# Attention block of a hybrid decoder layer: five query tiles one after another, where three were interleaved

## The reference, cut to what matters

```
s  = relu(qi @ ki^T)                       # 16 index heads of width 64
sc = sum_h wi[h] * s[h];  causal           # index score of each key
idx = top_k(sc, 128)                       # 128 keys are kept per query
p  = softmax(q @ k^T + bias[distance])     # 4 heads of width 128, kept keys only
o_a = p @ v
x  = x + concat(o_a, o_b, o_c) @ w_out     # this block does the o_b, o_c rows
```

## Time and profile before

| | us |
|---|---|
| median of 3 runs | 3632.32 (3630.06 to 3635.02) |
| profiled execution | 3625.24 |
| its span | 3623.4 |
| this block in the trace | 1682 to 1943.7 |
| attention on DVE | 1719.7 to 1943.7 |

### The profile page before, as it was taken

How to read it: one execution, slowest core, us unless ns; L and a number is a source line. 1 busy time by engine, 2 the same in 40 slices (tenths; PEclk the granted TensorE clock), 3 DMA queues, 4 the chain that set the end, 5 groups by cost and what they waited for, 6 DMA issues and landing times. The chain is left out here.

```text
span 3623.4 us, 54272 instructions
## 1 busy us (share of the span) xinstructions
PE 3210.1 (89%) x22287; PEld 2955.0 (82%) x22287; DVE 2186.9 (60%) x3229; ACT 564.8 (16%) x1074; POOL 1419.0 (39%) x853
## 2 busy tenths in 40 slices
PE   7978997999993477783997999999999999999998
PEld 6935886899772377752886999999999999999998
DVE  7025994898318666446896755546555555555554
ACT  3222211122325211114321200000000000000000
POOL 4353332476323232313333444434444343444442
PEclk9989998999995698776998999999999999999999
DMA  5322332478643000217333222322323222222232
GB/s 181 95 78 83 107 88 77 128 218 253 204 143 102 17 1 1 54 51 206 96 99 135 67 91 83 94 83 85 91 82 94 82 91 83 87 85 89 83 94 97
DMA packets 415941, 360.30 MB, mean 99 GB/s; under 512 B 26362, under 2 KB 367962, under 8 KB 414309
## 3 DMA queue, kind: packets, MB, share of 16 engines
q1 hardware_dynamic: 379664, 287.06, 27.0%
q0 software_dynamic: 13440, 42.02, 3.6%
q10 hardware_dynamic: 22592, 27.59, 2.3%
HBM read 311.63 MB, written 46.20 MB: 99 GB/s over the span
## 5 line engine op out<-in xcount | busy, mean ns | idle before, releaser
L3067 POOL TENSOR_TENSOR om_ring<-om_raw,om_mask 128x1024 fp32r<-128x1024 f32 x264 | 680.7, 2579 | 937.2 <-DVE om_ring L3185 937.2
L3107 PE MATMUL om_ps<-om_h,om_ring 128*128 128x272 f32 x6144 | 780.3, 290 | 21.6 <-issue 18.1
L3107 PEld LDWEIGHTS om_ps<-om_h,om_ring 128*128 128x128 f32 x6144 | 777.6, 190 | 24.1 <-issue 23.9
L3107 PE MATMUL om_ps<-om_hid,om_ring 128*128 128x272 f32 x6144 | 770.6, 288 | 0.0
L3107 PEld LDWEIGHTS om_ps<-om_hid,om_ring 128*128 128x128 f32 x6144 | 769.8, 188 | 0.0
L3185 DVE CAST om_ring<-om_mask 128x1024 fp32r<-128x1024 f32 x264 | 455.2, 1724 | 9.1
L321 POOL TENSOR_TENSOR w_ring<-w_raw,w_mask 128x1024 fp32r<-128x1024 f32 (+2 forms) x110 | 259.5, 2378 | 370.5 <-DVE w_mask L452 210.3
L372 PE MATMUL pm_ps<-h,w_ring 128*128 128x280 f32 x2688 | 363.7, 297 | 26.2 <-issue 11.5
L372 PEld LDWEIGHTS pm_ps<-h,w_ring 128*128 128x128 f32 x2688 | 356.0, 193 | 33.7 <-issue 26.6
L3193 DVE TENSOR_TENSOR om_x<-om_x,om_ps 128x272 f32<-128x272 f32 x288 | 112.7, 433 | 357.8 <-PE om_ps L3107 354.5
L390 PE MATMUL pq_ps<-w_ring,h 128*128 128x512 f32 (+2 forms) x1440 | 291.3, 364 | 7.7 <-POOL w_ring L321 7.6
(11 more groups left out here) (521 smaller groups left out, 3668.9 us busy)
## 6 DMA issues: line engine op xcount, KB each, us to landing
om_raw<-in_w_up SPq DMA_DIRECT2D x128, 512.0 KB, 4.1
om_raw<-in_w_down SPq DMA_DIRECT2D x128, 512.0 KB, 3.6
w_raw<-in_w_in SPq DMA_DIRECT2D x112, 512.0 KB, 3.8
ao_raw<-in_w_out SPq DMA_DIRECT2D x32, 384.0 KB, 4.0
as_qb<-q_rows SPq DMA_DIRECT2D x32, 256.0 KB
projT<-pm_stage ACTq DMA_DIRECT2D x56, 140.0 KB
conv_x<-projT SPq DMA_DIRECT2D x28, 280.0 KB, 2.7
xT_scratch<-ln_xT SPq DMA_DIRECT2D x1, 4480.0 KB, 15.4
```

Of the source, the lines that this page charges most:

```text
L3067: pool.tensor_tensor(f32r(ring[:, s, 1, half_of(q)]), raw[:, q, :], mask[:, q, :], ALU.subtract).then_inc(split[q], 1)
L3107: ins = pe.matmul(ps[bank][:, 0:HM], w, f32r(src[:, b, k, kept_half(half)]), start=first, stop=last)
```

## The change

Attention goes through the tiles in sequence: on DVE the head sums of tile i, then its 16 selection rounds, then its four heads, then tile i + 1. The due times come from three tables of step lengths. The tile's phases begin at:

| tile | sums | selection | heads | next tile |
|---|---|---|---|---|
| 0 | 12 | - | 12 | 21 |
| 1 | 21 | 29 | 45 | 54.4 |
| 2 | 54.4 | 64.3 | 84.3 | 95.3 |
| 3 | 95.3 | 107.3 | 131.3 | 143.9 |
| 4 | 143.9 | 146.9 | 170.9 | 184.3 |

The index scores on PE are due 2.5 before the sums, the logits matmuls 2.5 before their use on DVE. The projection's streams keep their due times. Instructions, shapes and buffers are the same; only the order changes, on DVE, PE, ACT and POOL.

```diff
-AS_FROM, AS_PER = (12.0, 24.0, 50.5, 89.0, 122.5, 156.0), (0.75, 1.65, 2.4, 2.1, 2.1, 3.0)
+SUM_PER, TOP_PER, HEAD_PER = (0, 0.5, 0.62, 0.75, 0), (0, 1.0, 1.25, 1.5, 1.5), (1.5, 1.6, 2.0, 2.4, 2.6)
+SUM_FROM, TOP_FROM, HEADS_FROM = {}, {}, {}
+CLOCK = 12.0
+for TILE in range(5):
+    SUM_FROM[TILE] = CLOCK
+    TOP_FROM[TILE] = SUM_FROM[TILE] + HI * SUM_PER[TILE] + 3 * (TILE == 4)
+    HEADS_FROM[TILE] = TOP_FROM[TILE] + (TOPP // 8 * TOP_PER[TILE])
+    CLOCK = HEADS_FROM[TILE] + 4 * HEAD_PER[TILE] + 3
 def logits_at(i, h):
-    return when(0, 4 * h + 1.2) if i == 0 else when(i + 1, 4 * h + 1.7) if i < 4 else when(5, 1 + h)
+    return HEADS_FROM[i] + 2 + HEAD_PER[i] * h
 def weights_at(i, h):
-    return logits_at(i, h) + (1.5 if i == 0 else 2.8 if i == 4 else 2 * AS_PER[i + 1])
+    return logits_at(i, h) + HEAD_PER[i] + 0.5
...
-                    for r in range(TOPP // 8):
-                        yield when(i, r)
-                        step(dve.max(best[0:n, r % 2, :], x))
-                        step(dve.match_replace(x, best[0:n, r % 2, :], x, TAKEN))
-                        if i < 3:
-                            add_head(i + 1, r)
...
-                        if i >= 2 and r % 4 == 1:
-                            yield logits_at(i - 1, r // 4)
-                            logits(i - 1, r // 4)
-                        if i >= 2 and r % 4 == 3:
-                            yield weights_at(i - 1, r // 4)
-                            normalise(i - 1, r // 4)
...
+                    if i in (1, 2, 3):
+                        for h in range(HI):
+                            yield SUM_FROM[i] + SUM_PER[i] * h
+                            add_head(i, h)
+                            if h == 12:
+                                heads_out(i - 1)
+                    if i:
+                        for r in range(TOPP // 8):
+                            yield TOP_FROM[i] + TOP_PER[i] * r
+                            step(dve.max(best[0:n, r % 2, :], x))
+                            step(dve.match_replace(x, best[0:n, r % 2, :], x, TAKEN))
...
+                    yield logits_at(i, 0)
+                    logits(i, 0)
+                    for h in range(HA):
+                        if h + 1 < HA:
+                            yield logits_at(i, h + 1)
+                            logits(i, h + 1)
+                        yield weights_at(i, h)
+                        normalise(i, h)
```

More of the change, by code:

```diff
@@ L1737, in in_time @@
         due[who] = next(streams[who], None)
-AS_FROM, AS_PER = (12.0, 24.0, 50.5, 89.0, 122.5, 156.0), (0.75, 1.65, 2.4, 2.1, 2.1, 3.0)
+SUM_PER, TOP_PER, HEAD_PER = (0, 0.5, 0.62, 0.75, 0), (0, 1.0, 1.25, 1.5, 1.5), (1.5, 1.6, 2.0, 2.4, 2.6)
 FIRST_UNIT, UNIT = 2.0, 10.6
-def when(phase, r):
-    return AS_FROM[phase] + AS_PER[phase] * r
+SUM_FROM, TOP_FROM, HEADS_FROM = {}, {}, {}
[5 more added lines that the diff above has]
+    CLOCK = HEADS_FROM[TILE] + 4 * HEAD_PER[TILE] + 3
 def unit_at(n):
@@ L1796, in attend_and_project @@
         wide = ((0, slice(0, WIDE)), (1, slice(WIDE, TP)))
-        order = [(when(0, h) - 2.5, "i", 1, h) for h in range(HI)]
-        order += [(when(i - 1, h) - 2.5, "i", i, h) for i in (2, 3) for h in range(HI)]
-        order += [(when(3, 5), "w", 4, 0), (when(3, 6.5), "w", 4, 1), (when(3, 9), "s", 4, 0)]
+        order = [(SUM_FROM[i] + SUM_PER[i] * h - 2.5, "i", i, h) for i in (1, 2, 3) for h in range(HI)]
+        order += [(SUM_FROM[4] - 1.5, "w", 4, 0), (SUM_FROM[4] - 0.5, "w", 4, 1), (SUM_FROM[4] + 1.8, "s", 4, 0)]
         order = sorted(order + [(logits_at(i, h) - 2.5, "h", i, h) for i in range(5) for h in range(HA)])
@@ L2157, in inputs @@
                     step(dve.tensor_scalar(wi[0:NT[i], i, :], wi[0:NT[i], i, :], float(HI * DI) ** -0.5, None, ALU.mult))
-                yield when(1, 2)
+                yield SUM_FROM[2]
                 dve.wait_ge(s["wq_in"], 16 * 8)
@@ L2207, in attend @@
             def attend():
[L2208 to L2218, removed]
@@ L2219, in attend @@
-                for i in range(1, 5):
+                for i in range(5):
                     n = rows[i]
                     x = sc[0:n, i % 3, 0:keys[i]]
-                    for r in range(TOPP // 8):
-                        yield when(i, r)
-                        step(dve.max(best[0:n, r % 2, :], x))
-                        step(dve.match_replace(x, best[0:n, r % 2, :], x, TAKEN))
-                        if i < 3:
-                            add_head(i + 1, r)
[L2228 to L2238, removed]
-                        if i >= 2 and r % 4 == 1:
-                            yield logits_at(i - 1, r // 4)
-                            logits(i - 1, r // 4)
-                        if i >= 2 and r % 4 == 3:
-                            yield weights_at(i - 1, r // 4)
-                            normalise(i - 1, r // 4)
-                    step(dve.tensor_scalar(x, x, TAKEN, NEG, ALU.not_equal, ALU.mult))
-                    diag = sc[0:n, i % 3, P * i:keys[i]]
-                    dve.tensor_tensor(diag, diag, causal[0:n, 0:n], ALU.add).then_inc(s["mask_ready"], 1)
@@ L2248, in attend @@
[L2248 to L2256, removed]
+                    yield SUM_FROM[i] + 2.9 * (i == 4)
+                    if i == 0:
+                        dve.tensor_copy(sc[:, 0, 0:P], causal[:, :]).then_inc(s["mask_ready"], 1)
@@ new lines, in attend @@
+                    if i == 4:
+                        dve.wait_ge(s["score"], nth["s", 4, 0] + 1)
+                        dve.wait_ge(s["bm_ready"], HA * 2)
+                        for ps, part in both(("s", 4, 0)):
+                            ins = dve.tensor_copy(sc[0:TAILP, 1, part], ps[0:TAILP, 0:WIDE])
+                        ins.then_inc(s["sums_out"], 1)
+                        dve.wait_ge(s["sums_out"], 1)
+                        step(dve.tensor_tensor(x[:, 512:], x[:, 512:], causal[0:TAILP, 0:TAILP], ALU.add))
@@ new lines, in attend @@
+                    if i in (1, 2, 3):
[9 more added lines that the diff above has]
+                            step(dve.match_replace(x, best[0:n, r % 2, :], x, TAKEN))
+                            if i == 4 and r == 2:
+                                heads_out(3)
+                        step(dve.tensor_scalar(x, x, TAKEN, NEG, ALU.not_equal, ALU.mult))
+                        diag = sc[0:n, i % 3, P * i:keys[i]]
+                        dve.tensor_tensor(diag, diag, causal[0:n, 0:n], ALU.add).then_inc(s["mask_ready"], 1)
```

## The result

The changed kernel takes 3654.6 us (median of 5 runs) against 3632.3 (5 runs): ratio 1.0059, interval 1.0048 to 1.0071, so **22.3 us slower**. I had forecast slower by 9.3 us (3641.6). The sign held and so did the range (3629 to 3655), its upper end by 0.4 us; the size was 2.4 times too small.

A forecast was written before the change was run, and what follows sets the result against it. PE and DVE, both nearly full, bounded the block together; in sequence each phase takes its slower engine's time. Phases and tail summed to 233.3 us against 224.0, +9.3 on the 3632.32 median: 3641.6, range 3629 to 3655.

The forecast's parts named there:

- the walk: Step through PE's and DVE's lists over the attention block: 233.3 us instead of 224.0, +9.3; chance 0.48.
- DVE's stop at tile 4: DVE stands about 9 us at its wait for tile 4's sums (L2232).
- the first rival: PE's lead absorbs DVE's lag after selections 1 to 3, saving up to 11 us; 3625 to 3636; chance 0.32.
- the signs that I had named: Trace checks, including DVE's selection 4 starting at 1908 and PE's last weights about 10 us earlier than 1940.
- the tail: After selection 4 only tile 4's heads remain: 17.1 us to the end; bounds 13 with overlap, 20 at lower clock.
- the second rival: PE's stops at four phase changes lower its clock, 2 to 3 us each; tail's PE steps double; 3654; chance 0.13.
- Heads 0 with sums 1: Block start, tile 0's heads then tile 1's head sums: +9.8 and +13.4 us on DVE.
- Heads 1: Tile 1's heads after its selection: +10.4 us, PE waiting 1.3 at the third logits, 0.7 and 1.6 at turns.
- heads 2: Tile 2's heads after its selection: +10.8 us, with PE waiting 2.9 and 1.3.
- The rule weighed in the prediction: Shared DVE/POOL SBUF ports: lows add up to 1.4 us to first normalise of tiles 1 and 2; total about +11.
- Selection 3: Tile 3's selection rounds, bound by DVE: 24.2 + 3.4 (masks and adds of two units) + 0.7 = 28.3 us.
- Heads 3 with tile 4's scores: Tile 3's heads and tile 4's scores: +26.7 us, PE waiting 3.3 and 5.0 behind the lows of unit 13.

The follow-up runs named there:

- e3: Changed kernel with projection weights planned unevenly, more in selections and fewer in sums and heads; ratio 1.0023 to the kernel before, attention 231.3 us against 246.2.
- e4: Changed kernel with tile i-1's heads back between tile i's selection rounds, sums still a separate phase; ratio 1.0013 to the kernel before, attention 227.2 us.
- e1: Changed kernel plus 84 unread weight matmuls on PE between the last weights and tile 4's heads; ratio 1.0046 to the kernel before, attention 242.2 us.
- e8: e1 plus 2, 3 and 5 unread matmuls before the third logits matmul of tiles 1, 2 and 3; ratio 1.0048 to the kernel before, attention 244.2 us.
- e6: e3 with POOL's bm of tiles 1 to 4 due 2.4 earlier; ratio 1.0045 to the kernel before, attention 238.4 us.
- e7: e4 with projection weights paced by phase, at other rates than e3; ratio 1.0013 to the kernel before, attention 226.9 us.
- e9: Changed kernel with POOL's lows of unit 13 moved ahead of tile 3's first bm; ratio 1.0059 to the kernel before, attention 243.9 us.

## Why the prediction was right, and where its size failed

**What held.** The model: phases with waits on both sides, each as long as its slower engine. Of the eleven windows, five came within 0.2 us of the walk: selections 1, 2 and 4 (17.9, 24.0, 28.0 for 18.0, 24.1, 27.9) and sums 2 and 3 (20.0 and 26.5 for 20.1 and 26.7). So did DVE's stop at tile 4 (9.1 for 9). PE does wait at the third logits matmul; the first rival, that its lead takes up the lag, asked for no wait there after selections 1 to 3 and is refuted by 10.5 us of it. e3 shows the sums to be PE's, e4 shows that phases of heads cost most of the loss.

Not all of this is skill. PE's waits up to the end of heads 3 come to 18.0 us for 16.6 in the walk, but in other places: 10.5 for 7.5 at the third logits matmuls, 3.7 for 8.6 at the turns of tiles 1 to 3, 3.4 for 0.5 in heads 0, and 0.4 at a relu. And two of the signs that I had named failed. Selection 4 starts at 1914.9 (1922.5 less 7.6), 6.9 us after 1908, and PE ends its weights at 1938.0, where I had 1931.

**What failed is a term of the sum: the tail**, 17.1 in the walk, 20 at the lower clock as its bound, and 23.0 in the trace. That is 5.9 of the 12.9 us that are missing. I had written that PE would end the weights early, that is, that it would stand before the tail, and had kept the price of the clock for the second rival and as a bound. It belonged in the walk, since PE's early end was part of it. e1 gives 3.9 us for the clock and e8 2.0, each a part of its price. The 2.0 by which e1's tail still exceeds the walk lie behind the last normalise, 5.4 us for about 3.5. There the last turn waits 1.3 us behind the values of the head before, a place in PE's list that I had not counted; the last values take 2.26 at the lower clock where I had 1.8; and four unread matmuls stand between. How much the order alone costs in the changed kernel no run separates.

The second rival named two places for the clock. It was right about the tail ("PE steps double") and, as far as the runs show, wrong about the size at the changes of phase, 2 to 3 us each: heads 1 gained 0.7 and heads 2 nothing on the changed kernel when their clock was full. Its time, 3654, is the measured one, by luck; half of its reason is not.

**Smaller terms** make up the rest. Their reasons are read from rows, and no experiment tests one by itself:

- Heads 0 with sums 1, +1.7. I gave 16 scores their weights and forgot that PE has tile 0's turns and values among them, 4 x 0.34 us by my own prices; that is the likely reason.
- Heads 1, +1.1, and heads 2, +1.4. Heads 1 in order of time, DVE beside POOL, and PE before its first turn:

```profile
1770.10 1.56 DVE L2129 TENSOR_SCALAR ao_mask<-ao_raw 128x768 uint32<-128x768 uint32 x2
1770.26 1.98 POOL L2103 TENSOR_TENSOR mix<-ao_toe,ao_sc 128x256 f32<-128x256 f32 x2 [7.63 <-DVE ao_sc L2239]
...
1772.21 3.61 POOL L2088 TENSOR_TENSOR ao_ring<-ao_raw,ao_mask 128x768 fp32r<-128x768 f32 x2
...
1774.04 1.93 DVE L2203 TENSOR_SCALAR mix<-mix,ao_den 128x256 f32<-128x256 f32 x1
...
1775.03 1.92 PE L1938 MATMUL ao_w<-ao_mh,ao_ring 128*128 128x272 f32 x6
...
1776.75 0.47 PE L1988 MATMUL ao_t<-ident,mix 128*128 128x128 f32 x2
...
1778.34 0.35 DVE L2203 TENSOR_SCALAR mix<-mix,ao_den 128x256 f32<-128x256 f32 x1
```

  The normalise takes 1.93 beside the lows and 0.35 without them, and the masks 1.56 beside `bm` where they take 1.03. I had allowed 0.5 for each. The rule weighed in the prediction (the Trainium skill, SBUF — State Buffer, "Who interferes with whom"), which asked for up to 1.4 more, agrees with this. But the delay was not what the first turn waited for. The normalise ended at 1775.97, and the turn came at 1776.75, behind six weights that took 1.92 at the lower clock. In e1, with the clock at 1.00, they took 1.10; the turn then waited 0.60 for the equally slow normalise, and heads 1 was 10.7. So of the 1.1, some 0.7 is the clock. In heads 2 the first normalise took only 0.75, but the masks before the second `logits` took 1.70 instead of 1.03. That is about half of the 1.4, and I have no experiment on the rest; e8, with the clock at 1.00 there, is no shorter.
- Selection 3, +0.9. The walk counted masks and adds of two units in it. The trace has three pairs of masks (at 1865.8, 1878.1 and 1890.4, 1.03 us each) and two pairs of adds, so one pair of masks more.
- Heads 3 with tile 4's scores, +2.3. The rows in order of time:

```profile
1893.63 1.27 POOL L2103 TENSOR_TENSOR mix<-ao_toe,ao_sc 128x512 f32<-128x512 f32 x1 [11.00 <-DVE ao_sc L2239]
1894.86 3.59 POOL L2088 TENSOR_TENSOR ao_ring<-ao_raw,ao_mask 128x768 fp32r<-128x768 f32 x2
...
1895.68 1.41 PE L1973 MATMUL ao_s<-ao_att 128*128 128x512 f32 x2 [4.45 <-DVE mix L2189]
...
1898.41 3.74 POOL L2103 TENSOR_TENSOR mix<-ao_toe,ao_sc 128x512 f32<-128x512 f32 x3
...
1899.72 0.69 DVE L2189 TENSOR_TENSOR mix<-ao_s,mix 128x512 f32<-128x512 f32 x1 [3.38 <-POOL mix L2103]
...
1902.49 0.66 PE L1988 MATMUL ao_t<-ident,mix 128*128 128x128 f32 x4 [2.68 <-DVE mix L2203]
...
1903.67 3.43 PE L1938 MATMUL ao_w<-ao_mh,ao_ring 128*128 128x272 f32 x12
...
1913.73 1.78 PE L1938 MATMUL ao_w<-ao_mh,ao_ring 128*128 128x272 f32 x12
```

  The order `bm`, lows, `bm` is as predicted, and the two waits of PE are 4.45 and 2.68 where I had 3.3 and 5.0: together less. What was missing is behind them: twelve weights take 3.43 us just after PE's waits and 1.78 ten us later. Some 1.6 us of clock lie there, in front of the next turn. That is read from the rows, and e8, whose clock stayed at 0.88 in this phase, does not test it.

**Where 22.2 us went**, then: 9.3 as the walk had it, 5.9 in the tail (2.0 to 3.9 of it clock, at the least), 7.0 in the smaller terms, for most of which the rows offer a reason. By cause instead of place, heads in phases of their own cost 19.0 in the trace (e4). Pacing the weights by phase takes 14.9 off (e3), of which some 8 stay when the lows stand between the `bm` again (e6). The two overlap: both together, in e7, take off 19.3, hardly more than e4 alone.

## What to carry to other kernels

When two engines are both near full in an interleaved stretch, putting its parts in sequence makes each phase as long as its slower engine; sum the maxima, phase by phase, and then look where filler work (here the weights) lies: it belongs in the phases in which its engine would stand. Ask of every engine that finishes its filler early what clock it will have in the chain of small steps that follows, and put that price in the sum, not in a rival. In lists that run in order, look for a long operation that falls between two short ones that others wait for; here moving all the short ones forward undid half of a gain, and a long one moved ahead of them delayed the step that they wait for. When an experiment gains more than its reason allows, look in its trace for what else moved, as the lows did in e3.

## What the runs showed of the hardware

PE was busy 17.31 of 23.00 us in the tail, in many small matmuls, and its granted clock was 0.50 all the same; it had stopped for 7.2 us before. In e1 it was busy 17.64 of 19.10 in the same steps with weights between, and had 0.88; in e8, with the same instructions, it was busy 19.90 of 20.80 and had 0.75. At 0.50 (1.2 GHz) ten matmuls of 16 columns with their weight loads took 2.43 us and at full speed (2.4 GHz) 1.28, so the time nearly doubles for such small ones too. Heads 1 and 3, with waits of 2.6 and 4.5 us at their start, had 0.85 and 0.88; sums 2 and 3 had 1.00 again. The wait alone does not settle it: in e1 heads 1, after the same 2.61 us, had 1.00.

A DVE step of 128x128 with both inputs in SBUF took 1.77 us beside POOL's lows and 0.29 without them (e9).
